# Top-k rounds over 136 candidate pairs, with key numbers found by a difference and a minimum of magnitudes

## The chip, the cores and the metric

The kernel runs on one core of one Trainium2 chip. The metric is the device time of one launch in microseconds. Engines are named as in the profile: PE is TensorE, DVE VectorE, ACT ScalarE, POOL GpSimd, SP SyncE. They run side by side, each in its own order, and meet at semaphores.

## The reference

One layer over 640 tokens of width 1024 (512 of a prompt, 128 of eight running streams) in float32. First a mixing half (a gated unit and a linear recurrence), then a retrieval half, in which each token picks experts by product keys. Of the retrieval, per head of eight:

```
v1, i1 = top_k(s1, 16)                  # s1, s2: 128 scores each
v2, i2 = top_k(s2, 16)
cand   = v1[:, None] + v2[None, :]      # 16 x 16 = 256 sums
cidx   = i1[:, None] * 128 + i2[None, :]
top_s, sel = top_k(cand, 16)
eidx   = cidx[sel];  g = softmax(top_s)
out   += sum_k g_k * gelu(u_tab[eidx_k] . x) * v_tab[eidx_k]
```

So each token has 8 x 16 = 128 expert numbers, and each number stands for a row of two tables of 16384 x 1024. Both lists v1 and v2 come sorted, largest first. A final norm follows.

## The kernel before

The tokens are five tiles of 128, worked in three "fronts": front 0 is tile 0 (the streams), front 1 tiles 1 and 2, front 2 tiles 3 and 4. Each front runs the mixing half (called I in the order), then "rounds" (II), which choose the expert numbers. Front 0 has 4 rounds, fronts 1 and 2 have 8 each, 20 in all. A round covers two heads of one tile or one head of two tiles, so always two groups ("units") of 128 tokens side by side along the free axis.

Once numbers are known, POOL gathers rows by indirect DMA into a ring of six places (line 614: a row of both tables, 8 KB per partition; line 616: a row of the first table alone, 4 KB). DVE takes dot products with the gathered rows (lines 892 and 903), ACT makes the coefficients, and the weighted sum goes to PE (line 1476) or to DVE (line 912). Tiles 1 and 2 are "dense": their second half runs over the whole second table, brought in 128 blocks of 512 KB by SP (line 568), against a coefficient matrix that is built by one-hot products (DVE lines 952 and 954, PE line 1450, multiplied at line 1461). For each half of that table 32 fills are followed by 64 blocks.

The order of all pieces is one list made by `weave` (due times written out by hand), and every engine goes through the list in that order. Each engine therefore does what is its own in a fixed sequence; a late piece holds all behind it on its engine.

A round has ten steps; step number `at` on DVE: 5 and 6 find the best sixteen of the scores for each unit (`best_keys`), 7 is `best_sums`, 8 is `next_sums`, 9 is `pick_numbers` and then `weights`. In front 0's first round the steps stand next to each other; elsewhere dot products and other pieces lie between them.

- `best_sums`: two instructions make the 256 sums of each unit (line 835). Then for each unit the eight largest (line 817), their places (820), and a copy with these taken out (823).
- `next_sums`: the next eight and their places, without line 823; the negated maximum (line 845), on which ACT's exponential and PE's score products of the next round wait; then the place is split into row and column (848, 849), and compared with 0 to 15 (851), which gives a 0/1 mask of 64 x 16 values.
- `pick_numbers`: the mask is multiplied by the key numbers (864), summed over 16 (867), and the two key numbers are put together to an expert number (870; also 875 for front 1). POOL waits for that.

`st.step` counts an instruction; `st.after` makes DVE wait until the last counted one has finished.

Of the kernel before, what the change touches and what calls it, by code (L numbers as in the profile page):

```python
# [7 lines left out]
U32 = mybir.dt.uint32  # L8
ALU = mybir.AluOpType
ACT = mybir.ActivationFunctionType  # L10
AX_X = mybir.AxisListType.X

P = 128
# [10 lines left out]
HEADS = 8  # L24
TOPK = 16
SLOTS = HEADS * TOPK
PAIRS = SLOTS // 2
RING = 6
DIAGS = 4
# [54 lines left out]
def weave():  # L84
# [8 lines left out]

    for s in range(SLOTS // 2):
        put.append((1.2 * s, ("dot", s)))
# [8 lines left out]
    b, u = 77.0, 0  # L104
    for i in range(SLOTS // 2):
        put.append((b, ("dot", SLOTS // 2 + i)))
        put.append((b + 1.11, ("mix", SLOTS // 2 + i)))
        b += 1.2
# [6 lines left out]
    put.append((b + 4.02, ("norm", 0)))  # L115
    while u < SLOTS:
        put.append((b, ("udot", u)))
# [169 lines left out]
def hybrid_layer(nc, x_all, cols, conv_state, lru_state, w_in, w_out, w_q, ws_t, w_a, w_i, keys_t, rows, experts,  # L287
                 y_all, v_rows, state_sample, state_prompt):
    with ExitStack() as ctx:
        def sb(name, shape, dt=F32):  # L290
            return ctx.enter_context(nc.sbuf_tensor(name, [P] + shape, dt))
# [29 lines left out]
        pick = sb("pick", [D])  # L321
# [13 lines left out]
        iota = sb("iota", [P])  # L335
# [14 lines left out]
        vals = sb("vals", [2, 2, TOPK])  # L350
        idx8 = sb("idx8", [2, 2, TOPK], U32)
        best = sb("best", [2, TOPK])
        sel = sb("sel", [2, TOPK], U32)
        selu = sb("selu", [2, 2, TOPK], U32)
        e12 = sb("e12", [2, 2, TOPK])
        nmax = sb("nmax", [2])
        gexp = sb("gexp", [2, TOPK])
# [8 lines left out]
        diag = sb("diag", [DIAGS, P])  # L366

        srow = pick[:, 0:2 * P].rearrange("p (e k) -> p e k", e=2)
        cand = pick[:, 0:512].rearrange("p (h k) -> p h k", h=2)
        left = pick[:, 512:1024].rearrange("p (h k) -> p h k", h=2)  # L370
        eqm = pick[:].rearrange("p (k a) -> p k a", a=TOPK)
        ws_s = pick[:, 0:GROUPS * P].rearrange("p (g n) -> p g n", g=GROUPS)

# [245 lines left out]
        def _(v):  # L619
            st = Steps(v, dve_step, dve_held)  # L620
            V = nc.vector
# [15 lines left out]
            for k in (15, 13, 11, 9, 7, 5, 3):  # L637
                v.wait_ge(dve_set, done)
                V.scalar_tensor_tensor(out=lt[:, 4], in0=lt[:, 4], scalar=1.0 / k, in1=lt[:, 3], op0=ALU.add,
                                       op1=ALU.mult).then_inc(dve_set, 1)  # L640
# [3 lines left out]
                                   op1=ALU.mult).then_inc(dve_set, 1)  # L644
# [4 lines left out]
                                   op1=ALU.add).then_inc(dve_set, 1)  # L649
# [182 lines left out]

            def best_sums():
                st.after()
                made = [st.step(V.tensor_tensor(cand[:, h].rearrange("p (a b) -> p a b", a=TOPK),
                                                vals[:, h, 0].unsqueeze(2).to_broadcast([P, TOPK, TOPK]),
                                                vals[:, h, 1].unsqueeze(1).to_broadcast([P, TOPK, TOPK]), ALU.add))
                        for h in range(2)]
                top_eight(0, [cand[:, 0], cand[:, 1]], [best[:, 0], best[:, 1]], [sel[:, 0], sel[:, 1]],
                          [left[:, 0], left[:, 1]], made)  # L840

            def next_sums(f, r):
                top_eight(1, [left[:, 0], left[:, 1]], [best[:, 0], best[:, 1]], [sel[:, 0], sel[:, 1]], None,
                          [st.last, st.last])
                guard = st.gives(V.tensor_scalar(nmax[:], best[:, :, 0], -1.0, None, ALU.mult), best_done,
                                 ROUND_BASE[f] + r + 1)
                v.wait_ge(*guard)
                st.step(V.tensor_scalar(selu[:, :, 0], sel[:], 4, None, ALU.logical_shift_right))
                st.step(V.tensor_scalar(selu[:, :, 1], sel[:], TOPK - 1, None, ALU.bitwise_and))
                st.after()  # L850
                st.step(V.tensor_tensor(eqm, selu[:].rearrange("p h e k -> p (h e k)").unsqueeze(2).to_broadcast(
                    [P, 4 * TOPK, TOPK]), iota[:, 0:TOPK].unsqueeze(1).to_broadcast([P, 4 * TOPK, TOPK]), ALU.is_equal))

            def by_unit(t, f, r):

# [3 lines left out]
                return t[:, a:a + 2, r * TOPK:(r + 1) * TOPK]  # L859

            def pick_numbers(f, r):
                eq4 = eqm.rearrange("p (q k) a -> p q k a", q=4)
                st.after()
                st.step(V.tensor_tensor(eq4, eq4, idx8[:].rearrange("p h e a -> p (h e) a").unsqueeze(2).to_broadcast(
                    [P, 4, TOPK, TOPK]), ALU.mult))
                st.after()
                st.step(V.tensor_reduce(e12[:].rearrange("p h e k -> p (h e k)"), eqm, AX_X, ALU.add))
                st.after()
                out = eid[:] if f == 1 else by_unit(idc, f, r)
                ins = V.scalar_tensor_tensor(out=out, in0=e12[:, :, 0], scalar=float(P), in1=e12[:, :, 1], op0=ALU.mult,  # L870
                                             op1=ALU.add)
                if f == 1:
                    st.step(ins)
                    st.after()
                    ins = V.tensor_scalar(by_unit(idc, f, r), eid[:], 2.0, None, ALU.mult)
                st.gives(ins, idx_ready, ROUND_BASE[f] + r + 1)
# [672 lines left out]
```

## Time and profile before

| | us |
|---|---|
| three runs, median | 1841.43 (1837.32 to 1843.55) |
| profiled execution, its time | 1844.83 |
| profiled execution, its span | 1842.6 |
| PE busy | 1470.5 (80%) |
| DVE busy | 1464.2 (79%) |
| POOL busy | 783.0 (42%) |
| ACT busy | 635.5 (34%) |
| HBM read | 671.61 MB |

Busy time is the sum of the instructions of an engine. The page has, beside it, the span cut into 40 slices of 46 us with each engine's busy share, the granted clock of PE and the DMA rate; the costliest groups of instructions; and the chain that ended last, followed back from the last instruction to what released it each time. Several engines are near four fifths busy, so the stretches have to be looked at one by one.

### The profile page before, as it was taken

To read this page: it belongs to the slowest core of one execution; us is meant where nothing else is said; L and a number is where in the kernel's file an instruction comes from. 1 tells how busy PE (TensorE), PEld (TensorE's weight loads), DVE (VectorE), ACT (ScalarE), POOL (GpSimd) and SP (SyncE) were. 2 spreads that over 40 slices of the span, in tenths; PEclk is the share of its full clock that TensorE was granted. 3 is DMA by queue.
4 is the path that set the end of the run, shared out by engine and by line. 5 is a ranking of instruction groups with operands and counts; after the bars stand their busy time and mean duration, and the time that the engine had idled before them with its cause. 6 is when DMAs were issued, how large, how long until landed. Compare 5 with 4: busy or idle time off the path is not lost.

```text
span 1842.6 us, 17478 instructions
## 1 busy us (share of the span) xinstructions
PE 1470.5 (80%) x4706; PEld 797.9 (43%) x4706; DVE 1464.2 (79%) x2979; ACT 635.5 (34%) x1935; POOL 783.0 (42%) x667
## 2 busy tenths in 40 slices
PE   6799796666666651976868999899998888999997
PEld 5485343433333210733745555333334555433332
DVE  1278788999998969769999989997667989766665
ACT  4335534222222221250037877221114667311111
POOL 2023233475776668748733334322222444422220
PEclk9899898887777785988979999999999888999999
DMA  9389999899999999999979989999998999999996
GB/s 353 144 325 409 373 353 375 317 376 381 399 379 394 365 409 371 392 344 366 406 277 331 344 313 350 418 417 417 417 417 335 362 351 370 400 417 417 417 417 250
DMA packets 146482, 675.78 MB, mean 367 GB/s; under 512 B 15216, under 2 KB 15472, under 8 KB 97232
## 3 DMA queue, kind: packets, MB, share of 16 engines
q0 software_dynamic: 92832, 538.39, 74.8%
q1 hardware_dynamic: 50496, 132.68, 18.7%
q10 hardware_dynamic: 3056, 3.61, 0.6%
q8 instruction: 37, 0.61, 0.1%
q14 instruction: 61, 0.50, 0.1%
HBM read 671.61 MB, written 3.01 MB: 366 GB/s over the span
## 4 chain that ended last, share of the span: by engine, by line
DMA 30%; PE 29%; DVE 21%; issue 10%; ACT 7%; POOL 2%; ACTq 0%; DVEq 0%; POOLq 0%; SPq 0%
DMA arena<-experts 20%; DMA ring<-experts,idc 10%; PE accY L1476 7%; PE pb L1461 7%; DVE ring L903 6%; PE pb L1281 4%; DVE ring L892 4%; PE pb L1290 2%; PE pb L1450 2%; ACT arena L1206 2%; PE pq L1407 2%; PE pb L1299 2%; DVE arena L952 2%; PE pb L1306 2%; POOL ring L616 1%
## 5 line engine op out<-in xcount | busy, mean ns | idle before, releaser
L614 POOL DMA_INDIRECT ring<-experts,idc x384 | 445.7, 1161 | 892.3 <-DVE xt L912 393.3
L1476 PE MATMUL accY<-ring,diag 128*128 128x512 f32 x792 | 458.9, 715 | 217.9 <-ACT diag L1192 217.6
L892 DVE CUSTOM_DVE_ANT_0 ring<-ring,h 128x1024 f32<-128x1024 f32 x384 | 466.6, 1222 | 194.3 <-DMA ring<-experts,idc 193.5
L1461 PE MATMUL pb<-arena 128*128 128x512 f32 x1024 | 473.0, 607 | 21.0 <-DMA arena<-experts 14.4
L616 POOL DMA_INDIRECT ring<-experts,idc x256 | 327.1, 1278 | 121.4 <-issue 76.0
L1181 ACT ACTIVATE ge<-zt 128x1 f32<-128x1 f32 x384 | 76.7, 200 | 790.9 <-DVE zt L892 789.3
L1476 PEld LDWEIGHTS accY<-ring,diag 128*128 128x128 f32 x792 | 160.3, 220 | 431.8 <-ACT diag L1192 294.5
L1461 PEld LDWEIGHTS pb<-arena 128*128 128x128 f32 x1024 | 186.3, 191 | 306.1 <-issue 196.4
L912 DVE SCALAR_TENSOR_TENSOR xt<-ring,coef,xt 128x1024 f32<-128x1024 f32 x186 | 238.4, 1282 | 6.5 <-ACT coef L1185 6.4
L1407 PE MATMUL pq<-arena 128*128 128x256 f32 (+1 forms) x768 | 153.2, 360 | 8.8 <-ACT arena L1176 4.7
L903 DVE CUSTOM_DVE_ANT_0 ring<-ring,arena 128x1024 f32<-128x1024 f32 x128 | 152.9, 1220 | 8.5 <-DMA ring<-experts,idc 7.9
L903 DVE CUSTOM_DVE_ANT_0 ring<-ring,h 128x1024 f32<-128x1024 f32 x128 | 151.5, 1221 | 8.1 <-DMA ring<-experts,idc 7.0
L1206 ACT ACTIVATE arena<-arena,qT 128x64 f32<-128x64 f32 x512 | 129.1, 334 | 80.5 <-DVE arena L954 80.5
L1450 PEld LDWEIGHTS pb<-arena 128*128 128x128 f32 x1024 | 131.6, 201 | 40.5 <-issue 31.6
L1407 PEld LDWEIGHTS pq<-arena 128*128 128x128 f32 x768 | 134.2, 204 | 34.4 <-issue 19.8
L1450 PE MATMUL pb<-arena 128*128 128x64 f32 x1024 | 128.1, 281 | 3.9 <-ACT arena L1206 3.9
L1185 ACT ACTIVATE coef<-ge,gc 128x1 f32<-128x1 f32 x384 | 113.3, 295 | 12.6
L952 DVE TENSOR_TENSOR arena<-iota,qT 128x1024 f32<-128x1024 f32 x64 | 78.1, 1221 | 14.7 <-PE pb L1450 14.7
L1192 ACT ACTIVATE diag<-ident,coef 128x128 f32<-128x128 f32 x198 | 79.6, 402 | 6.5
L1271 PE MATMUL pb<-ident,arena 128*128 128x128 f32 x100 | 18.9, 362 | 74.2 <-ACT arena L1044 53.5
L1281 PE MATMUL pb<-arena 128*128 128x256 f32 (+1 forms) x384 | 74.3, 357 | 3.3 <-ACT arena L1051 3.3
L1290 PE MATMUL pb<-arena 128*128 128x512 f32 x144 | 66.1, 616 | 6.3 <-ACT arena L1093 6.3
(174 smaller groups left out, 1123.8 us busy)
## 6 DMA issues: line engine op xcount, KB each, us to landing
arena<-experts SPq DMA_DIRECT2D x128, 512.0 KB, 15.1
arena<-w_q SPq DMA_DIRECT2D x12, 2048.0 KB, 19.5
arena<-w_in SPq DMA_DIRECT2D x11, 2048.0 KB, 20.7
ring<-experts,idc POOLq DMA_INDIRECT x640, 9.2
arena<-w_out SPq DMA_DIRECT2D x4, 2048.0 KB, 21.0
ring<-w_out SPq DMA_DIRECT2D x2, 2048.0 KB, 21.6
xt<-x_all SPq DMA_DIRECT2D x5, 512.0 KB, 13.5
y_all<-xt ACTq DMA_DIRECT2D x5, 512.0 KB, 3.5
```

The source lines that it names most:

```text
L614: nc.gpsimd.indirect_dma_start(ring[:, at // 2], None, experts, index).then_inc(gat[at], 16)
L616: nc.gpsimd.indirect_dma_start(half(g), None, halves, index).then_inc(gat[at], 16)
L892: V.tensor_tensor_reduce(out=half(g), in0=half(g), in1=h2[:], scale=1.0, scalar=0.0, op0=ALU.mult, op1=ALU.add, accum_out=zt[:, s % 8:s % ...
L903: V.tensor_tensor_reduce(out=half(g), in0=half(g), in1=h, scale=1.0, scalar=0.0, op0=ALU.mult, op1=ALU.add, accum_out=zd[:, u:u + 1]).then ...
L912: V.scalar_tensor_tensor(out=x, in0=ring[:, PLACE["whole", s][0] // 2, D:2 * D], scalar=coef[:, s % 8:s % 8 + 1], in1=x, op0=ALU.mult, op1 ...
L952: V.tensor_tensor(hot2[:, k % 2], iota[:].unsqueeze(1).to_broadcast([P, BATCH, P]), idT[:, 1, a].unsqueeze(2).to_broadcast([P, BATCH, P]), ...
L1206: ins = A.activation(hot1[:, k % 2, i], hot1[:, k % 2, i], ACT.Copy, scale=idT[:, 2, n * BATCH + i:n * BATCH + i + 1])
L1281: ins = T.matmul(pflat[:, o:o + w], wt[:, c, m * P:(m + 1) * P], hT[:, c, 0:w], start=c == 0, stop=c == DC - 1)
L1407: ins = T.matmul(pq[:, q * w:(q + 1) * w], wt[:, c, o:o + P], h2T[:, c, 0:w], start=c == 0, stop=c == DC - 1)
L1450: ins = T.matmul(pb[:, k % 4, i * BLOCKS:(i + 1) * BLOCKS], hot2[:, k % 2, i], hot1[:, k % 2, i], start=True, stop=True)
L1461: ins = T.matmul(pb[:, 2 * j + k], cm[:, i, j * P:(j + 1) * P], vring[:, n % VRING, k * 512:(k + 1) * 512], start=i == 0, stop=i == BLOCKS ...
L1476: ins = T.matmul(accY[:, j], diag[:, (n - 1) % DIAGS], ring[:, place, D + j * 512:D + (j + 1) * 512], start=first, stop=final)
```

## The change

The sums of a unit are cut from 256 to 136 columns: 16 for the largest v1 with all v2, and 8 for each of the other fifteen v1 with the first eight v2. A sum at row a and column b (from 0) can be among the sixteen largest only where (a + 1)(b + 1) is at most 16. The place in this list is split differently, and the key number is found in another way: each key number is stored with 256 times its row added (`tagged`), the wanted row times 256 is subtracted, and of the sixteen differences the one of the smallest magnitude is the key number.

```diff
+CANDS = TOPK + (TOPK - 1) * 8
+        row8 = sb("row8", [2, 2, TOPK], U32)
+        tagged = sb("tagged", [4, TOPK])
-        cand = pick[:, 0:512].rearrange("p (h k) -> p h k", h=2)
-        left = pick[:, 512:1024].rearrange("p (h k) -> p h k", h=2)
+        cand = pick[:, 0:2 * CANDS].rearrange("p (h k) -> p h k", h=2)
+        left = pick[:, 512:512 + 2 * CANDS].rearrange("p (h k) -> p h k", h=2)
 best_sums:
-                made = [st.step(V.tensor_tensor(cand[:, h].rearrange("p (a b) -> p a b", a=TOPK),
-                                                vals[:, h, 0].unsqueeze(2).to_broadcast([P, TOPK, TOPK]),
-                                                vals[:, h, 1].unsqueeze(1).to_broadcast([P, TOPK, TOPK]), ALU.add))
-                        for h in range(2)]
+                st.step(V.tensor_tensor(cand[:, :, 0:TOPK], vals[:, :, 0, 0].unsqueeze(2).to_broadcast([P, 2, TOPK]),
+                                        vals[:, :, 1], ALU.add))
+                made = st.step(V.tensor_tensor(
+                    cand[:, :, TOPK:].rearrange("p h (a b) -> p h a b", b=8),
+                    vals[:, :, 0, 1:].unsqueeze(3).to_broadcast([P, 2, TOPK - 1, 8]),
+                    vals[:, :, 1, 0:8].unsqueeze(2).to_broadcast([P, 2, TOPK - 1, 8]), ALU.add))
+                made = [made, made]
 next_sums, behind the negated maximum:
-                st.step(V.tensor_scalar(selu[:, :, 0], sel[:], 4, None, ALU.logical_shift_right))
-                st.step(V.tensor_scalar(selu[:, :, 1], sel[:], TOPK - 1, None, ALU.bitwise_and))
+                st.step(V.tensor_scalar(row8[:, :, 0], sel[:], 0xF8, 5, ALU.bitwise_and, ALU.logical_shift_left))
+                st.step(V.tensor_scalar(row8[:, :, 1], sel[:], 7, 8, ALU.bitwise_and, ALU.logical_shift_left))
+                st.step(V.scalar_tensor_tensor(out=tagged[:], in0=iota[:, 0:TOPK].unsqueeze(1).to_broadcast(
+                    [P, 4, TOPK]), scalar=256.0, in1=idx8[:].rearrange("p h e a -> p (h e) a"), op0=ALU.mult,
+                    op1=ALU.add))
                 st.after()
-                st.step(V.tensor_tensor(eqm, selu[:].rearrange("p h e k -> p (h e k)").unsqueeze(2).to_broadcast(
-                    [P, 4 * TOPK, TOPK]), iota[:, 0:TOPK].unsqueeze(1).to_broadcast([P, 4 * TOPK, TOPK]), ALU.is_equal))
+                st.step(V.tensor_scalar(selu[:, :, 0], row8[:, :, 0], 256.0, 256.0, ALU.max, ALU.subtract))
+                st.step(V.tensor_scalar(selu[:, :, 1], row8[:, :, 0], 256.0, 2048.0, ALU.is_equal, ALU.mult))
+                st.after()
+                st.step(V.tensor_tensor(selu[:, :, 1], selu[:, :, 1], row8[:, :, 1], ALU.bitwise_or))
+                st.after()
+                st.step(V.tensor_tensor(eqm.rearrange("p (q k) a -> p q k a", q=4),
+                                        tagged[:].unsqueeze(2).to_broadcast([P, 4, TOPK, TOPK]),
+                                        selu[:].rearrange("p h e k -> p (h e) k").unsqueeze(3).to_broadcast(
+                                            [P, 4, TOPK, TOPK]), ALU.subtract))
 pick_numbers:
-                eq4 = eqm.rearrange("p (q k) a -> p q k a", q=4)
                 st.after()
-                st.step(V.tensor_tensor(eq4, eq4, idx8[:].rearrange("p h e a -> p (h e) a").unsqueeze(2).to_broadcast(
-                    [P, 4, TOPK, TOPK]), ALU.mult))
-                st.after()
-                st.step(V.tensor_reduce(e12[:].rearrange("p h e k -> p (h e k)"), eqm, AX_X, ALU.add))
+                st.step(V.tensor_reduce(e12[:].rearrange("p h e k -> p (h e k)"), eqm, AX_X, ALU.min,
+                                        apply_absolute_value=True))
```

The order list, the gathers, the fills and all other pieces are the same in both kernels.

## Rows read from the trace of the kernel before

**Rows 1.** The page: busy time of the engines, DMA rate in 40 slices.

```profile
PE 1470.5 (80%) x4706; PEld 797.9 (43%) x4706; DVE 1464.2 (79%) x2979; ACT 635.5 (34%) x1935; POOL 783.0 (42%) x667
...
GB/s 353 144 325 409 373 353 375 317 376 381 399 379 394 365 409 371 392 344 366 406 277 331 344 313 350 418 417 417 417 417 335 362 351 370 400 417 417 417 417 250
```

**Rows 2.** Stretches: us, busy PE PEld DVE ACT POOL, PE clock, DMA share, GB/s.

```profile
109.00:345.00 236.00, 195.65 (x678) 117.42 (x678) 192.09 (x445) 100.91 (x256) 74.07 (x65) 0.91 0.95 372
345.00:640.00 295.00, 187.91 (x433) 92.04 (x431) 274.89 (x724) 72.47 (x205) 207.26 (x151) 0.77 0.98 377
860.00:950.00 90.00, 67.30 (x292) 56.76 (x293) 85.79 (x207) 9.42 (x17) 59.52 (x50) 0.86 1.00 389
950.00:1150.00 200.00, 180.37 (x798) 112.38 (x797) 185.83 (x428) 145.26 (x503) 77.41 (x62) 0.95 0.87 318
1150.00:1255.00 105.00, 97.20 (x227) 40.61 (x226) 102.39 (x232) 24.70 (x78) 31.13 (x28) 0.98 1.02 417
1255.00:1400.00 145.00, 140.54 (x306) 54.54 (x305) 92.97 (x115) 23.35 (x82) 37.06 (x38) 1.00 1.02 417
```

**Rows 3.** DVE groups by form: out<-in xcount, busy us, mean ns, idle before.

```profile
L912 DVE SCALAR_TENSOR_TENSOR xt<-ring,coef,xt 128x1024 f32<-128x1024 f32 x186 | 238.4, 1282 | 6.5 <-ACT coef L1185 6.4
...
L820 DVE FIND_INDEX8 sel<-best,pick 128x8 uint32<-128x256 f32 x80 | 32.5, 419 | 0.0
...
L817 DVE MAX8 best<-pick 128x8 f32<-128x256 f32 x80 | 29.9, 416 | 0.3
...
L820 DVE FIND_INDEX8 idx<-vals,psc 128x8 uint32<-128x128 f32 x80 | 22.3, 291 | 0.6 <-issue 0.6
...
L823 DVE MATCH_REPLACE8 pick<-vals,psc 128x128 f32<-128x128 f32 x80 | 21.9, 281 | 0.0
L817 DVE MAX8 vals<-pick 128x8 f32<-128x128 f32 x80 | 21.1, 290 | 0.5 <-DVE vals L817 0.5
...
L823 DVE MATCH_REPLACE8 pick<-best,pick 128x256 f32<-128x256 f32 x40 | 16.1, 409 | 0.0
L835 DVE TENSOR_TENSOR pick<-vals 128x256 f32<-128x256 f32 x40 | 15.1, 419 | 0.1
...
L849 DVE TENSOR_SCALAR selu<-sel 128x32 uint32<-128x32 uint32 x20 | 4.6, 229 | 0.0
L882 DVE TENSOR_TENSOR gc<-gexp,gsum 128x32 f32<-128x32 f32 x20 | 3.9, 193 | 0.7
```

**Rows 4.** Timeline of DVE, end of front 0's first round: start us, us.

```profile
104.40 0.18 DVE L848 TENSOR_SCALAR selu<-sel 128x32 uint32<-128x32 uint32 x1
104.49 0.17 DVE L849 TENSOR_SCALAR selu<-sel 128x32 uint32<-128x32 uint32 x1
104.70 1.23 DVE L851 TENSOR_TENSOR pick<-selu,iota 128x1024 f32<-128x1024 uint32 x1
105.96 1.22 DVE L864 TENSOR_TENSOR pick<-pick,idx 128x1024 f32<-128x1024 f32 x1
107.22 1.22 DVE L867 TENSOR_REDUCE e<-pick 128x64 f32<-128x1024 f32 x1
```

**Rows 5.** The chain that ended last, pieces from four windows: start us, us.

```profile
99.62 0.48 DVE pick L835 x2
...
104.51 2.04 PE psc L1428 x8
...
928.07 1.15 DVE pick L864
...
1108.40 0.40 DVE pick L835 x2
```

**Rows 6.** Groups of POOL.

```profile
L614 POOL DMA_INDIRECT ring<-experts,idc x384 | 445.7, 1161 | 892.3 <-DVE xt L912 393.3 <-PE accY L1476 331.1 <-DVE idc L870 92.2
```

**Rows 7.** DVE's waits from 345 to 640 us: total us, times, longest.

```profile
DVE ring L892 <- DMA ring<-experts,idc: 10.4, 8, 2.0
```

**Rows 8.** DVE's waits from 860 to 1150 us.

```profile
DVE arena L952 <- PE pb L1450: 8.3, 4, 3.1
```

## The prediction

> **What bounds the kernel now.** The page comes first [rows 1]: TensorE (PE) and VectorE (DVE) are each busy for about four fifths of the span, and DMA moves 367 GB/s on average, so no engine alone sets the time. The changed code runs on DVE only, so the question is where DVE's time is the span's time. The view of busy time by stretches answers it [rows 2]. From 1150 on, and above all from 1255 to 1400, the DMA rate stands at 417 GB/s throughout while DVE is idle a third of the time: that is the transfers' ceiling here, and nothing that DVE saves is worth anything there. From 345 to 640 DVE is busy 274.9 of 295 us and DMA moves 377 GB/s, 10% under the ceiling: both are close. From 860 to 1150 DVE is busy 271.6 of 290 us, and from 950 on DMA is far below its ceiling (318 GB/s) while PE is busy 180 of 200. From 109 to 345 DVE (81%), PE (83%) and DMA (372 GB/s) share the work.
>
> Of the 20 rounds, 4 (front 0) run from 94 to about 300, 8 (front 1) from 323 to 630, and 8 (front 2) from about 900 to 1252, the last three of these after 1150. So 17 of 20 rounds lie where DVE can matter.
>
> Third, the chain of waits. I asked for each round whether its three changed parts lie on the chain that ended last: the sums with the first eight (best_sums), the second eight with what follows (next_sums), and the picking of numbers (pick_numbers). Their marks in the chain are lines 835, 845 and 864. Line 835 is on it 11 times, from the first round to the one at 1108; line 845 10 times; line 864 8 times, the last at 928 [rows 5]. After the last of these (1108) the chain lies on transfers, PE and the dot products, and no part of a round is on it.
>
> **What a round saves.** Durations are from [rows 3, 4].
>
> Searches over 136 columns in place of 256: the same instructions exist at 128 and at 256 columns. A MAX8 takes 290 and 416 ns, so 0.98 ns a column and 0.118 us less for 120 columns; FIND_INDEX8 291 and 419 ns, 0.120 us less; MATCH_REPLACE8 281 and 409 ns, 0.120 us less. best_sums has two of each, next_sums two of the first two: 0.72 and 0.48 us. The sums themselves: two of 256 elements (0.838 us) become one of 32 (193 ns, as line 882) and one of 240 (402 ns, by 16 columns less than 256 at the same slope): 0.24 us less. So best_sums saves 0.96 us, the first half of next_sums 0.48.
>
> The multiplication by the key numbers (line 864) goes: from its start to the next instruction's 1.26 us. The comparison becomes a subtraction of the same 1024 elements with an unsigned operand, 1.22 us as line 851; the sum becomes a minimum of magnitudes of the same 1024, for which I take line 867's 1.22 us. No row shows a minimum with magnitudes or a broadcast in four dimensions of such a subtraction; line 864 did its own four-dimensional broadcast at 1.22. From below the bound is no change (three different passes over 1024 elements all take the same 1.22 us, so I exclude a gain); from above line 912, a three-operand pass over 1024 elements with a scalar read from memory, takes 1.28 us, 0.06 more a pass and 0.12 for the two. I take zero, nearest to three equal rows.
>
> What is added: before, lines 848 and 849 stood between nmax and the comparison, 0.30 us from the first start to the comparison's start (the second starts 0.09 us after the first, as nothing waits between them). After, three instructions without a wait between them (two of 32 elements, one of 64, the last costing some 226 ns between line 882's 32 and line 835's 256), a wait, two of 32, a wait, one of 32, a wait: 0.44 + 0.31 + 0.22 = 0.97 us with 0.03 us for each wait. That is 0.67 us more, all in next_sums, so next_sums as a whole gets 0.19 us longer. Bounds: 0.5 if two-step instructions overlap further, 1.2 if each takes line 849's mean of 229 ns and none overlaps. The new waits are on DVE's own instructions; what is queued behind them is DVE's next dot product or piece, and for it the price is counted already.
>
> Sum for a round: 0.96 + 0.48 - 0.67 + 1.26 = 2.03 us, and 40.6 us of DVE over 20 rounds. No transfer, PE or ACT instruction is added or taken away. ACT's exponentials hang on nmax, which comes 1.44 us earlier.
>
> **One thing that speaks against it.** Line 849 takes 0.17 us in the first round, before any gather, and 229 ns on average [rows 3, 4]: some of these short instructions are held, and GpSimd, which issues the gathers, is busy 42% of the span [rows 1]. The excess is 0.06 us each, so 40 more such instructions (four in a round where two were) cost at most 2.4 us in all; half of that, 0.06 us a round, I leave out as too small to matter. GpSimd's gather instruction has 1.16 us [rows 6]. The Trainium skill (SBUF — State Buffer, Who interferes with whom) says that such a scalar operation from SBUF to SBUF can take a port pair that GpSimd shares, and that whoever comes second waits for the whole instruction. By that rule at its worst, an estimate with half of that gather instruction as the wait: 40 x 0.42 x 0.58 = 10 us. The rows are at a quarter of it or less.
>
> **What of it is on the path.** Line 835's parts 11 x 0.96 = 10.6; line 845's 10 x 0.48 = 4.8, less 9 x 0.67 = 6.0 (after the first round's maximum PE takes the chain over at 104.51, so its tail is not on it); line 864's 8 x 1.26 = 10.1. Together 19.4 us. By stages: 2.0 in front 0's rounds, 2.0 in front 1's first (323 to 344), 9.9 between 345 and 640 (three, three and six marks), 5.5 in front 2's (five, three and one).
>
> Not all of that will be had, because what is next is near. Between 345 and 640 DVE already waits 10.4 us for gathers in line 892 alone [rows 7]; where a gain exceeds the slack of the transfers in flight, the wait for them grows instead. The transfers' own floor is 295 x (1 - 377/417) = 28 us below, so they take a share, not the whole. From 860 to 1150 DVE waits 8.3 us for PE's fills [rows 8] and PE has 20 us of idle time in the 200 from 950, over twice what four rounds save there, but in pieces. In front 0's stage PE has the chain at once after the first round. I take two thirds: 13 us. The tail from 1150 on is bytes at 417 GB/s and keeps its length, so 13 us earlier there is 13 us earlier at the end. The profiled execution has a span of 1842.6 and a time of 1844.8 us, 0.2% above the median 1841.4 of the runs; 1844.8 - 13 = 1831.8, and against the median 1828. Measurement can't tell less than about 0.3% (5.5 us) from no change.
>
> **Rivals.**
>
> *The transfers pace the middle.* DVE's waits from 345 to 640 grow by all it saves and the stretch gives nothing. For it: the page's 46 us slices reach 399 GB/s there, near the ceiling. Against: others are at 317 and 365 [rows 1], and DVE, 93% busy, is what else could hold them. What is left is 19.4 - 9.9 = 9.5, two thirds of it 6.4: 1835. The Trainium skill (DMA: Bandwidth & Descriptors, Where 436 GB/s comes from) says that HBM to SBUF traffic is held at about 358 GB/s for a core; by that the stretch would be over its limit already and this rival certain. The 417 GB/s of [rows 2] contradict that figure here.
>
> *All of DVE's time counts.* If DVE alone paces everything before 1150, its idle time being knock-on waits on itself, 17 x 2.03 = 34.5 us come off: 1807. For it: 94% busy between 860 and 1150. Against: its real waits for gathers and for PE.
>
> *Slower by TensorE's clock.* From 950 to 1150 the granted clock is 0.95 of 2.4 GHz and PE is busy 180 of 200 us; from 345 to 640, where PE mostly waits for DVE, it is 0.77. If the shifted order of DVE's pieces lets PE pause more at the start of the fills and it then runs there at 0.77, PE's work becomes 180 x 0.95/0.77 = 222 us, and the stretch takes 22 us more, against 13 saved: 1841 + 22 - 13 = 1850. It decides from a mean clock of 0.855 down (180 x 0.95/200). Against: less DVE work gives PE less to wait for.
>
> **How the numbers follow.** Forecast 1828, chance 0.60, its own range 1820 to 1835. The transfers' pace 0.22 (1835; a third of its cases within 0.3%). All of DVE's time 0.12. The slower clock 0.06. Faster by over 0.3%: 0.58 + 0.15 + 0.12 = 0.85; within: 0.09; slower: 0.06. The range for 8 of 10 leaves out most of the 34 us case and the slower one: 1813 to 1838. It holds the small costs' upper bound too (0.53 + 0.12 us more a round, some 17 x 0.65 x 2/3 = 7 us: 1835).
>
> **What would show it.** MAX8 and FIND_INDEX8 over the sums at 0.30 us; line 864's 24.4 us gone and DVE's busy time 41 us lower, near 1424; the short group 1.0 us from nmax's end to the subtraction; the minimum at 1.22 us. The middle stretch above 377 GB/s. The chain's hand-over to the transfers of the V blocks, now near 1150, some 13 us earlier and the length from there to the end the same 693 us. If that length changes by more than 3 us, or DVE's saved time turns up whole as waits for gathers, the prediction is wrong in its mechanism.

## The result and the profile after

Eight runs of the changed kernel have a median of 1827.24 us (1819.6 to 1831.73), against 1842.41 us for the kernel before on the same chip (1836.55 to 1847.77, eight runs): ratio 0.993, 95% interval 0.9907 to 0.9953, so faster, clear of noise. Measured once more (e9, six runs) it has 1826.89 us, ratio 0.9913 (0.9884 to 0.9943). The ratios here and below are those on record and not the quotients of the medians given beside them, which would be 0.9918 and 0.9917; by the first ratio the change gained 13 us, by the medians 15. The forecast was 1828 us. That figure came out right partly because errors in its terms offset each other, as the stages show.

The page after: busy time, and the rate of the transfers in 40 slices (the lines of [rows 1]).

```profile
PE 1470.6 (80%) x4706; PEld 800.0 (44%) x4706; DVE 1427.7 (78%) x3039; ACT 634.3 (35%) x1935; POOL 783.3 (43%) x667
...
GB/s 356 146 334 410 375 354 382 336 397 399 398 384 399 368 416 361 372 357 388 405 277 307 353 335 358 418 416 417 416 418 351 345 366 370 383 417 417 417 416 263
```

DVE's busy time fell by 36.5 us, PE's, ACT's and POOL's did not move. The slices of the middle stretch (the eighth to the fourteenth) rose from 317 to 399 GB/s to 336 to 399; the plateau at 417 is where it was.

Stretches after (columns as in [rows 2]):

```profile
345.00:640.00 295.00, 192.47 (x436) 95.11 (x436) 264.47 (x737) 73.90 (x210) 208.91 (x155) 0.78 0.99 389
...
950.00:1150.00 200.00, 180.87 (x796) 112.10 (x796) 180.92 (x455) 144.46 (x498) 78.12 (x66) 0.96 0.92 343
1150.00:1255.00 105.00, 102.07 (x241) 42.77 (x240) 91.67 (x213) 20.46 (x68) 30.55 (x28) 1.00 1.02 417
```

Against [rows 2] the middle stretch moves 389 GB/s in place of 377 with DVE 10 us less busy; from 1150 to 1255 the rate is the same 417 and DVE simply idles more. These windows stand at fixed times, so after the change they hold somewhat later work; cut at the same instructions (the marks below), the middle stretch goes from 376 to 386 GB/s.

DVE's groups by form after (columns as in [rows 3]):

```profile
L869 DVE TENSOR_TENSOR pick<-tagged,selu 128x1024 f32<-128x1024 f32 x20 | 24.7, 1237 | 0.7
L884 DVE TENSOR_REDUCE e<-pick 128x64 f32<-128x1024 f32 x20 | 24.2, 1212 | 0.0
...
L825 DVE FIND_INDEX8 sel<-best,pick 128x8 uint32<-128x136 f32 x80 | 22.5, 294 | 0.0
...
L822 DVE MAX8 best<-pick 128x8 f32<-128x136 f32 x80 | 20.0, 292 | 3.2
...
L828 DVE MATCH_REPLACE8 pick<-best,pick 128x136 f32<-128x136 f32 x40 | 11.1, 284 | 0.0
...
L842 DVE TENSOR_TENSOR pick<-vals 128x240 f32<-128x240 f32 x20 | 8.0, 401 | 0.0
...
L865 DVE TENSOR_SCALAR selu<-row 128x32 uint32<-128x32 uint32 x20 | 5.0, 252 | 0.0
```

And front 0's first round after, the timeline of DVE from the sums on (columns as in [rows 4]):

```profile
99.35 0.19 DVE L840 TENSOR_TENSOR pick<-vals 128x32 f32<-128x32 f32 x1
99.46 0.40 DVE L842 TENSOR_TENSOR pick<-vals 128x240 f32<-128x240 f32 x1
100.01 0.50 DVE L822 MAX8 best<-pick 128x8 f32<-128x136 f32 x2
...
102.78 0.15 DVE L853 TENSOR_SCALAR nmax<-best 128x2 f32<-128x2 f32 x1
102.96 0.18 DVE L858 TENSOR_SCALAR row<-sel 128x32 uint32<-128x32 uint32 x1
103.06 0.17 DVE L859 TENSOR_SCALAR row<-sel 128x32 uint32<-128x32 uint32 x1
103.14 0.22 DVE L860 SCALAR_TENSOR_TENSOR tagged<-iota,idx 128x64 f32<-128x64 f32 x1
103.39 0.18 DVE L864 TENSOR_SCALAR selu<-row 128x32 uint32<-128x32 uint32 x1
103.48 0.17 DVE L865 TENSOR_SCALAR selu<-row 128x32 uint32<-128x32 uint32 x1
103.69 0.19 DVE L867 TENSOR_TENSOR selu<-selu,row 128x32 uint32<-128x32 uint32 x1
103.92 1.23 DVE L869 TENSOR_TENSOR pick<-tagged,selu 128x1024 f32<-128x1024 f32 x1
105.18 1.22 DVE L884 TENSOR_REDUCE e<-pick 128x64 f32<-128x1024 f32 x1
106.43 0.19 DVE L888 SCALAR_TENSOR_TENSOR idc<-e 128x32 int32<-128x32 f32 x1
```

From the sums' first start to the start of the instruction that makes the expert numbers this is 106.43 - 99.35 = 7.08 us. Before, it was 8.85: the timeline of DVE there begins the sums at 99.62,

```profile
99.62 0.76 DVE L835 TENSOR_TENSOR pick<-vals 128x256 f32<-128x256 f32 x2
100.30 0.75 DVE L817 MAX8 best<-pick 128x8 f32<-128x256 f32 x2
```

and makes the numbers 1.25 us behind [rows 4], at 108.47. So this round saves 1.77 us, not 2.03. (It is the one round whose steps stand next to each other; 20 times 1.77 is 35.4 us, near the 36.5 us that DVE's busy time fell.) The step that was mis-sized is the sums: from the first start to the first MAX8 it was 0.68 us before and is 0.66 after. The busy time fell by 0.24 us, as forecast, but before, the first MAX8 waited only for its own unit's sums while the second unit's were being made; after, one instruction makes both units' sums and both MAX8 wait for its end.

**Where in the kernel the time came from.** The engines go through one written order, so the same instruction can be found in both timelines. Five marks on DVE, before:

```profile
343.81 0.19 DVE L870 SCALAR_TENSOR_TENSOR eid<-e 128x32 f32<-128x32 f32 x1
...
629.92 0.19 DVE L870 SCALAR_TENSOR_TENSOR eid<-e 128x32 f32<-128x32 f32 x1
...
954.52 1.22 DVE L952 TENSOR_TENSOR arena<-iota,qT 128x1024 f32<-128x1024 f32 x1
...
1139.35 1.22 DVE L952 TENSOR_TENSOR arena<-iota,qT 128x1024 f32<-128x1024 f32 x1
```

and after:

```profile
338.68 0.19 DVE L888 SCALAR_TENSOR_TENSOR eid<-e 128x32 f32<-128x32 f32 x1
...
615.60 0.19 DVE L888 SCALAR_TENSOR_TENSOR eid<-e 128x32 f32<-128x32 f32 x1
...
941.98 1.22 DVE L970 TENSOR_TENSOR arena<-iota,qT 128x1024 f32<-128x1024 f32 x1
...
1123.74 1.22 DVE L970 TENSOR_TENSOR arena<-iota,qT 128x1024 f32<-128x1024 f32 x1
```

They are the end of front 1's first and of its last round, and the first and the last one-hot product of the first half of the table. The fifth mark is the start of the last norm, 1837.5 and 1821.8. How much earlier each mark comes than before, in us, here and in the experiments (one profiled execution each):

| mark, time before | 343.8 | 629.9 | 954.5 | 1139.4 | end |
|---|---|---|---|---|---|
| changed kernel | 5.1 | 14.3 | 12.5 | 15.6 | 15.7 |
| changed kernel, again (e9) | 4.7 | 14.8 | 16.3 | 17.8 | 18.5 |
| only the minimum (e1) | 2.7 | 9.6 | 10.1 | 9.2 | 10.8 |
| only 136 columns (e2) | -0.2 | 2.1 | 3.2 | 4.8 | 3.4 |
| longer in front 1 (e3) | 2.4 | -2.9 | -3.9 | -1.8 | -2.0 |
| longer in front 2 (e4) | 5.5 | 16.2 | 18.7 | 9.5 | 13.4 |
| longer after 1150 (e5) | 3.9 | 11.7 | 11.5 | 14.2 | 19.0 |
| shorter in front 1 (e6) | 6.3 | 20.2 | 22.6 | 26.2 | 29.2 |
| shorter in front 2 (e7) | 4.2 | 14.0 | 16.3 | 25.5 | 25.2 |
| one instruction moved (e8) | 4.8 | 16.8 | 21.0 | 27.8 | 27.0 |
| 8 sums on DVE (e10) | 4.4 | 14.4 | 13.3 | 7.4 | 9.0 |
| 16 sums on DVE (e11) | 6.4 | 16.9 | 15.9 | 4.8 | 9.2 |

Six of these kernels (the changed one twice, e4, e5, e7, e10) have the same rounds up to 900 us (e7's first round of front 2, before the mark at 954, is already 2.3 us shorter). Among them the mark at 344 differs by 1.6 us, the one at 630 by 4.5, the one at 954 by 7.2: so much is chance from one execution to the next. Their means are 4.6, 14.2 and 14.8 us. All marks are taken against one execution of the kernel before, whose 1844.83 us is 2.4 above the median, so they show some 2 us too much in all. Read with that width, 4.6 us were won up to 344, 9.6 from there to 630, about nothing from 630 to 954, 2 to 3 from 954 to 1139 (3.1, 1.5 and, in e5, 2.7), and after it 0.1 and 0.7 in the two executions of the changed kernel. That last part scatters too: in e5 it is 4.8.

### The profile page after: what moved, and what is told of

Read it like the earlier page. It is cut to its first block, busy times and chain, and to the rows that moved or that the text cites. A ratio compares the mean times of both kernels' runs of the same rounds, so it can differ in the third digit from the quotient of the medians.

```text
span 1826.9 us, 17538 instructions
## 1 busy us (share of the span) xinstructions
PE 1470.6 (80%) x4706; PEld 800.0 (44%) x4706; DVE 1427.7 (78%) x3039; ACT 634.3 (35%) x1935; POOL 783.3 (43%) x667
## 4 chain that ended last, share of the span: by engine, by line
PE 32%; DMA 29%; DVE 19%; issue 10%; ACT 7%; POOL 2%; DVEq 0%; POOLq 0%; SPq 0%
DMA arena<-experts 18%; DMA ring<-experts,idc 10%; PE pb L1479 9%; PE accY L1494 8%; DVE ring L921 5%; PE pb L1299 4%; DVE ring L910 3%; PE pb L1468 2%; PE pb L1308 2%; PE pq L1425 2%; ACT arena L1224 2%; DVE arena L970 2%; PE pb L1317 2%; PE pb L1324 2%; POOL ring L621 1%
## 5 line engine op out<-in xcount | busy, mean ns | idle before, releaser
L1479 PE MATMUL pb<-arena 128*128 128x512 f32 x1024 | 473.5, 608 | 19.1 <-DMA arena<-experts 12.2
L1479 PEld LDWEIGHTS pb<-arena 128*128 128x128 f32 x1024 | 186.9, 191 | 304.1 <-issue 197.4
L921 DVE CUSTOM_DVE_ANT_0 ring<-ring,arena 128x1024 f32<-128x1024 f32 x128 | 153.4, 1220 | 11.5 <-DMA ring<-experts,idc 10.4
L921 DVE CUSTOM_DVE_ANT_0 ring<-ring,h 128x1024 f32<-128x1024 f32 x128 | 151.7, 1223 | 11.8 <-DMA ring<-experts,idc 10.9
L1468 PEld LDWEIGHTS pb<-arena 128*128 128x128 f32 x1024 | 132.6, 203 | 41.5 <-issue 31.1
L1203 ACT ACTIVATE coef<-ge,gc 128x1 f32<-128x1 f32 x384 | 113.2, 295 | 12.6
L1299 PEld LDWEIGHTS pb<-arena 128*128 128x128 f32 x384 | 66.8, 204 | 13.0 <-issue 4.4
```

The costliest lines, as they stand in the source:

```text
L921: V.tensor_tensor_reduce(out=half(g), in0=half(g), in1=h, scale=1.0, scalar=0.0, op0=ALU.mult, op1=ALU.add, accum_out=zd[:, u:u + 1]).then ...
L1299: ins = T.matmul(pflat[:, o:o + w], wt[:, c, m * P:(m + 1) * P], hT[:, c, 0:w], start=c == 0, stop=c == DC - 1)
L1468: ins = T.matmul(pb[:, k % 4, i * BLOCKS:(i + 1) * BLOCKS], hot2[:, k % 2, i], hot1[:, k % 2, i], start=True, stop=True)
L1479: ins = T.matmul(pb[:, 2 * j + k], cm[:, i, j * P:(j + 1) * P], vring[:, n % VRING, k * 512:(k + 1) * 512], start=i == 0, stop=i == BLOCKS ...
```

## The experiments

All ratios are to the kernel before on the same chip, medians with 95% intervals. "Pass" is one instruction over 1024 elements.

### e1: only the finding by a minimum

```diff
# against the changed kernel: sums and searches at 256 columns as before, and
+ st.step(V.tensor_scalar(selu[:, :, 0], sel[:], 0xF0, 4, ALU.bitwise_and, ALU.logical_shift_left))
+ st.step(V.tensor_scalar(selu[:, :, 1], sel[:], TOPK - 1, 8, ALU.bitwise_and, ALU.logical_shift_left))
- # the two row8 instructions, the two selu instructions and the bitwise_or
```

> The sums stay at 256 columns; only the finding of key numbers is changed (key numbers with 256 times their row added, one subtraction, one minimum of magnitudes). In a round one pass over 1024 elements goes (1.26 us from start to start) and the short group grows by one instruction (0.13 us): 1.13 us of VectorE a round, 22.6 in all. Theory A (a microsecond of VectorE saved before 1150 us is had at about 0.45 of what 20 rounds save, as the whole change gave 15.2 us for 20 x 1.77 = 35.4): 9.7 us faster than before. Rival B (both parts are needed before anything moves, or the searches carry it all): under 4 us. Rival C (VectorE paces all up to 1150 us): 17 rounds x 1.13 = 19 us.

1836.99 us, ratio 0.9973 (0.9943 to 1.0003): about 5 us faster, an interval that touches no change. Theory A's 9.7 us lies inside the interval and so does rival B's "under 4", so the time does not choose between them; rival C's 19 us is out. From nmax to the subtraction it has 0.61 us (0.48 before), so its saving of 1.13 us a round is as worked out. Its profiled execution was one of its faster ones (1834.01 us against the median of 1836.99), and its mark at 630 is 9.6 us earlier.

### e2: only the 136 columns

```diff
# against the changed kernel: no tagged; iota256 = 256 * (0 to 15), made once
- st.step(V.tensor_tensor(eqm..., tagged..., selu..., ALU.subtract))
+ st.step(V.tensor_tensor(eqm, selu..., iota256..., ALU.is_equal))
- st.step(V.tensor_reduce(e12..., eqm, AX_X, ALU.min, apply_absolute_value=True))
+ st.step(V.tensor_tensor(eq4, eq4, idx8..., ALU.mult))
+ st.after()
+ st.step(V.tensor_reduce(e12..., eqm, AX_X, ALU.add))
```

> The sums are cut to 136 columns; key numbers are found as before with a 0/1 mask, a multiplication and a sum (three passes over 1024 elements), but from the new places. VectorE saves 1.15 us in the searches and 0.02 in the sums and pays 0.52 for splitting the places: 0.65 us a round, 13.0 in all. Theory A: 5.6 us faster than before, and e1's and this one's gains add up to the whole change's 15. Rival B (the searches carry it): 11 us or more. Rival C (VectorE paces all up to 1150 us): 17 x 0.65 = 11 us, e1 then at 19.

1838.72 us, ratio 0.9969 (0.9949 to 0.9989): 5.7 us faster by the ratio (3.1 by the medians), as theory A had it. Its first round, from the sums to the expert numbers, takes 8.21 us against 8.85, 0.64 less. The two ratios together, 0.27% and 0.31%, make 0.58%, and the whole change has 0.7 to 0.87%; within the intervals they add up. Theory C, 19 and 11 us, is out, and so is the rival that the searches carry it all. The sizes by time are too near each other's intervals to say which part gives more. By DVE's time it is the minimum (1.13 against 0.65 us a round). The marks say the same, but e1's are those of one of its faster executions and e2's of one of its slower ones (1841.42 us).

### e3 and e6: more and less of DVE in front 1's rounds

e3 repeats the last pass twice more in each round of front 1; e6 leaves out the subtraction and the minimum there and takes the first sixteen key numbers of both lists as they stand. So e6 does not compute the layer's result: it gathers other rows of the tables, as many and as large. That their places in memory play no part is assumed.

```diff
# e3, behind the minimum:
+ for _ in range(2 if f == 1 else 0):
+     st.after()
+     st.step(V.tensor_reduce(e12..., eqm, AX_X, ALU.min, apply_absolute_value=True))
# e6:
+ if f == 1:
+     return                                     # ahead of the subtraction, which is left out
...
+ if f == 1:
+     st.step(V.tensor_copy(e12..., idx8...))    # in place of the minimum
```

> The changed kernel with front 1's eight rounds made longer: the last pass of each (the minimum over 1024 elements) is done three times, 2 x 1.25 us more a round, 20 us of VectorE between 340 and 630 us. Theory A (VectorE paces the middle stretch for about three quarters of its time, as the change gained 9.2 of 7 x 1.77 = 12.4 us there): 15 us slower than the changed kernel, so within 4 us of before. Rival T (transfers pace the middle stretch): under 4 us slower than the changed kernel. Rival C (VectorE paces it all): 20 us slower than the changed kernel, 5 slower than before.

> The changed kernel without the choice of the key numbers in front 1: the subtraction and the minimum over 1024 elements are left out, and the first sixteen key numbers of both lists are paired as they stand (so other rows of the tables are gathered, as many and as large). VectorE saves 2.3 us more a round, 18.5 in all. Theory A (the transfers' floor is near: 389 of 417 GB/s between 345 and 640 us, at most 20 us to be had): about half, 9 us faster than the changed kernel. Rival T (transfers pace it already): under 3 us. Rival C: 18 us.

e3: 1844.98 us, ratio 1.0011 (0.999 to 1.0032), so some 15 us slower than the changed kernel by the first ratio and 18 by the medians, as theory A had it; rival T's "under 4" is out. e6: 1816.92 us, ratio 0.9869 (0.9845 to 0.9893), some 10 us faster than 1827. But e5 and e8, which were measured together with e6 and do the changed kernel's work but for a late dose and a moved instruction, have 1822.43 and 1823.18 us; against them e6 is only some 6 us faster. Theory A had 9 and rival T under 3, and the time lies between. With the marks, from 344 to 630 (seven rounds):

- e3 adds 7 x 2.5 = 17.5 us of DVE to the changed kernel and the stretch gets 14.5 us longer (9.2 won becomes 5.3 lost): 0.83 a microsecond.
- the change itself took 12.4 us from the kernel before and won 9.2: 0.74.
- e6 takes another 16.1 us away and wins 4.7: 0.29.

Each of these is one execution. The six with the same rounds spread over 2.9 us in this stretch, so a slope is good to about 0.2; the fall to 0.29 is clear of that, the step between 0.83 and 0.74 is not.

The waits of DVE in that stretch, 345 to 640, for e3,

```profile
DVE ring L914 <- DMA ring<-experts,idc: 11.0, 9, 2.7
```

for the changed kernel,

```profile
DVE ring L910 <- DMA ring<-experts,idc: 19.0, 19, 2.3
```

and for e6,

```profile
DVE ring L916 <- DMA ring<-experts,idc: 30.4, 31, 2.8
```

show where time that DVE no longer needs turns up. The fixed window again holds later work in the faster kernels. Between the marks themselves DVE's waits for gathers (this line and the second dot product's, line 903 in the kernel before) are 15.8 us before, 16.0 in e3, 17.1 in the changed kernel and 28.1 in e6: 11.0 more in e6, which with the 4.7 won nearly makes up the 16.1 that it saved. The stretches themselves, e3 first, show the rate going from 374 to 400 GB/s (389 in the changed kernel):

```profile
345.00:640.00 295.00, 189.02 (x422) 94.57 (x422) 274.97 (x750) 71.15 (x200) 199.65 (x149) 0.73 0.98 374
```

```profile
345.00:640.00 295.00, 194.36 (x444) 94.17 (x444) 254.03 (x736) 75.53 (x215) 201.94 (x159) 0.80 1.01 400
```

So the price of a microsecond of DVE there is no constant. It bends where DVE starts to wait for gathers, and the change sits before the bend. The rate is then near the 417 GB/s of [rows 2]; whether that ceiling or the six places of the ring hold the gathers there, no run separates. The rival that the transfers already pace the middle is out for the change, but not for much more than it. (e3 is also a warning on DVE's busy column: at 274.97 it equals that of the kernel before.)

### e4 and e7: more and less of DVE in front 2's rounds

```diff
# e4, behind the minimum:
+ for _ in range(4 if f == 2 and 1 <= r <= 4 else 0):
+     st.after()
+     st.step(V.tensor_reduce(e12..., eqm, AX_X, ALU.min, apply_absolute_value=True))
# e7: as e6, with f == 2
```

> The changed kernel with four of front 2's rounds made longer (the second to the fifth, between 950 and 1150 us): the last pass is done five times, 4 x 1.25 us more a round, 20 us of VectorE. Theory A (PE is the limit there as often as VectorE: the change gained about 2 us of 7 there): some 10 us slower than the changed kernel, with VectorE's waits for PE's fills down from 24 us. Rival C (VectorE paces it): 20 us slower. Rival P (PE paces it alone): under 4 us slower.

> The changed kernel without the choice of the key numbers in front 2 (as e6, for the third front; five of its eight rounds before 1150 us): VectorE saves 2.3 us more a round, 11.5 before 1150. Theory A (PE limits the stretch from 950 to 1150 us): 2 to 4 us faster than the changed kernel, the rest turning into VectorE's waits for PE's fills. Rival C: 11 us faster.

e4: 1833.88 us, ratio 0.9957 (0.9938 to 0.9976); e7: 1821.53 us, ratio 0.988 (0.9852 to 0.9908). (e7, like e6, does not compute the layer's result.) Against the changed kernel's 1827 that is some 7 us slower and 6 faster; against e5 and e8, measured together with e7, it is only some 1 to 2 faster. The stretch between the marks at 954 and 1139 is the surer measure (us, one execution each):

| | length | DVE busy | DVE's waits for PE's fills |
|---|---|---|---|
| before | 184.8 | 172.2 | 8.3 |
| changed kernel | 181.8 | 164.8 | 12.9 |
| changed kernel, again (e9) | 183.4 | 164.9 | 14.2 |
| e3, e5, e6 | 182.7, 182.1, 181.2 | 165.0, 164.8, 165.4 | 11.7, 15.0, 8.4 |
| e8 | 178.0 | 164.0 | 9.3 |
| e4 | 194.0 | 184.3 | 4.3 |
| e7 | 175.7 | 156.2 | 12.7 |

e3, e5 and e6 have the changed kernel's rounds there, so five executions have the same work, 182.2 us on average. The change's own 4 x 1.77 = 7.1 us brought 2.6. As far as the one execution of the kernel before tells, most of the rest is in the last column: the wait for fills [rows 8] rose from 8.3 to 12.4 us on average. e4's 20 us more cost 11.8, 0.6 a microsecond, and the wait fell to 4.3: DVE did part of the added work in time in which it had waited. e7's 4 x 2.3 = 9.2 us less brought 6.6, 0.7 a microsecond, and the wait stayed. So the fills do take a share, as theory A had it for e4; for e7 it had 2 to 4 us and more waits, and that isn't seen. How far single executions can be off is shown by e8: with one instruction moved its stretch is 4 us shorter. The lines of the wait, 860 to 1150 us as in [rows 8], for the changed kernel,

```profile
DVE arena L970 <- PE pb L1468: 12.9, 6, 4.2
```

and for e4:

```profile
DVE arena L974 <- PE pb L1472: 6.0, 5, 1.7
```

### e5: more of DVE after 1150 us

```diff
# behind the minimum:
+ for _ in range(3 if f == 2 and r >= 5 else 0):
+     st.after()
+     st.step(V.tensor_reduce(e12..., eqm, AX_X, ALU.min, apply_absolute_value=True))
```

> The changed kernel with front 2's last three rounds made longer (after 1150 us, where the transfers run at 417 GB/s): the last pass is done four times, 3 x 1.25 us more a round, 11.2 us of VectorE. Theory A (transfers alone set the time there): no change against the changed kernel, within 2 us in the length from 1150 us to the end. Rival C (VectorE is busy 92 of 105 us there and its order holds the ring's places): up to 11 us slower.

1822.43 us, ratio 0.9891 (0.987 to 0.9911): 11.2 us more of DVE in these three rounds cost nothing. The stretch:

```profile
1150.00:1255.00 105.00, 102.52 (x245) 44.19 (x244) 103.65 (x232) 22.51 (x74) 29.54 (x28) 1.00 1.02 417
```

DVE is busy 103.65 of 105 us, more than in any other kernel here, and the rate is the same 417 GB/s. The busiest engine of a stretch isn't its limit when the transfers run at their ceiling. One part of the expectation failed: the length from the hand-over to the transfers of the second table's blocks (at 1134.22 us in the changed kernel) to the end, expected within 2 us of the changed kernel's 692.7, is 688.0. Over all kernels here it runs from 688.0 to 694.1. Nor is that tail all transfers at the ceiling: the page has slices of 335 to 370 GB/s in it before [rows 1], where the second half's fills are made, and the first to the last one-hot product of that half takes 167.6 to 174.7 us (169.0 before). e5's rounds say nothing about what DVE's time is worth there.

### e8: one instruction moved

```diff
- st.step(V.scalar_tensor_tensor(out=tagged[:], ...))        # ahead of the two selu instructions
- st.step(V.tensor_scalar(selu[:, :, 1], row8[:, :, 0], 256.0, 2048.0, ALU.is_equal, ALU.mult))
- st.after()
+ split = st.step(V.tensor_scalar(selu[:, :, 1], row8[:, :, 0], 256.0, 2048.0, ALU.is_equal, ALU.mult))
+ st.step(V.scalar_tensor_tensor(out=tagged[:], ...))
+ v.wait_ge(*split)
```

> The changed kernel with one instruction moved: the adding of 256 times the row to the key numbers goes behind the two instructions that split the places, where VectorE would wait. 0.14 us less a round from the negated maximum to the subtraction (0.96 to 0.82), 2.8 us of VectorE in all. Theory A: 1 to 2 us faster than the changed kernel, too little to tell by time, to be seen in the timeline of the first round. Rival B (the gap is not a wait but the start of the next instruction): no difference in the timeline.

1823.18 us, ratio 0.9902 (0.988 to 0.9924), not to be told from the changed kernel by time. The timeline of its first round:

```profile
101.75 0.18 DVE L858 TENSOR_SCALAR row<-sel 128x32 uint32<-128x32 uint32 x1
101.84 0.17 DVE L859 TENSOR_SCALAR row<-sel 128x32 uint32<-128x32 uint32 x1
102.05 0.18 DVE L861 TENSOR_SCALAR selu<-row 128x32 uint32<-128x32 uint32 x1
102.14 0.17 DVE L862 TENSOR_SCALAR selu<-row 128x32 uint32<-128x32 uint32 x1
102.23 0.22 DVE L863 SCALAR_TENSOR_TENSOR tagged<-iota,idx 128x64 f32<-128x64 f32 x1
102.36 0.18 DVE L867 TENSOR_TENSOR selu<-selu,row 128x32 uint32<-128x32 uint32 x1
102.58 1.22 DVE L869 TENSOR_TENSOR pick<-tagged,selu 128x1024 f32<-128x1024 f32 x1
```

From the first splitting to the subtraction it is 0.83 us, against 0.96 in the changed kernel: the gap was a wait, and an independent instruction fits into it.

### e9, e10, e11: is PE the limit between 954 and 1139?

e9 is the changed kernel again, as the neighbour of the other two. They move weighted sums of tile 3 from PE to DVE.

```diff
 def by_vector(s):
-    return k >= SLOTS // 2 or (t == 2 and k % 5 in (1, 3))
+    return k >= SLOTS // 2 or (t == 2 and k % 5 in (1, 3)) or (t == 1 and k % 8 == 3)   # e10
+    return k >= SLOTS // 2 or (t == 2 and k % 5 in (1, 3)) or (t == 1 and k % 4 == 3)   # e11, on e8
```

> The changed kernel as it is, once more, so that the next kernels have it beside them on the same chip. From its first measurement: 0.993 of before, about 13 us; from the three kernels that differ least from it (a late dose, a moved instruction) 0.989 to 0.990. I expect 0.990 to 0.993.

> The changed kernel with 8 of the first 64 weighted sums of tile 3 (between 950 and 1150 us, every eighth) moved from PE to VectorE: PE gives up 8 x 1.73 = 13.8 us there, VectorE takes on 8 x 1.28 = 10.2 us. Theory P (PE's matmuls limit that stretch; e4 put 20 us more on VectorE there for some 5 to 7 us): 4 to 10 us faster than the changed kernel. Rival V (VectorE limits it as much): no change or up to 10 us slower. Rival L (the chain of one-hot, scaling and fill limits it, not the sums): no change.

> As e10 with 16 sums moved (every fourth), and the adding of the row moved behind the splitting as in e8: PE gives up 27.7 us between 950 and 1150, VectorE takes on 20.5. Theory P: VectorE is now the limit; about as e10 or a few us worse, 0 to 8 us faster than the changed kernel. Rival V: 10 to 20 us slower.

e9: 1826.89 us, 0.9913 (0.9884 to 0.9943), as expected. e10: 1833.14 us, 0.9951 (0.9933 to 0.997). e11: 1834.42 us, 0.9946 (0.9921 to 0.9971). Theory P, which was mine, falls: neither got faster. Rival L's "no change" isn't seen either. Rival V fits e10, 6 us slower than e9; for e11 it had 10 to 20, and by time e11 is 7.5 slower, though its stretch is 13 to 14 longer. The stretch between the two marks, for the changed kernel, e10 and e11:

```profile
942.00:1123.80 181.80, 167.56 (x745) 105.00 (x746) 164.86 (x399) 136.67 (x478) 68.82 (x58) 0.96 0.88 324
```

```profile
941.20:1131.90 190.70, 163.68 (x719) 103.74 (x720) 174.11 (x406) 134.89 (x473) 73.59 (x58) 0.91 0.83 310
```

```profile
938.60:1134.60 196.00, 161.32 (x689) 104.62 (x690) 182.34 (x414) 132.40 (x466) 69.35 (x58) 0.87 0.83 307
```

10.2 us more on DVE made it 8.9 us longer (7.3 against e9). In e11, of whose 16 sums 15 lie between the marks, 19.2 us made it 14.2 longer (12.6 against e9, but 17.9 against e8, whose order of instructions it has). PE gave up 13.8 and 27.7 us of matmuls by the price of one at full clock, but its busy time fell by 3.9 and 6.2 us only: its mean clock, the last number but two of a line, went from 0.96 to 0.91 and 0.87. So PE at 92% busy was not the limit by its matmuls: taking some away and putting less on DVE made the stretch longer, by about what e4's dose on DVE alone would (0.6 a microsecond there, 0.7 to 0.9 here). DVE is the limit for most of its time. No run takes work from PE alone, and whether the lower clock, by slower fills, has a part in the longer stretch is not separated.

## Why the prediction was right, and where its terms were not

- **The limit by stretches: shown.** Added time on DVE counts for most of itself from 344 to 630 (e3), for 0.6 and more between 954 and 1139 (e4, e10), and for nothing in the three rounds after 1150 (e5).
- **Searches, 0.120 us an instruction: shown**, a little more (292, 294, 284 ns against 416, 419, 409 in [rows 3]).
- **The sums, 0.24 us: mis-sized.** 0.02 by starts. The overlap of two independent instructions with the first search was lost, and the forecast had subtracted busy times.
- **The two remaining passes at 1.22 us: shown** (1.237 and 1.212). The multiplication's 1.26 is gone.
- **The short group, 0.67 us more: shown** in the first round, 0.96 against 0.30. Over all rounds line 865 means 252 ns and line 864 207, against 0.17 and 0.18 in the first round. That is at most 0.08 us on an instruction (the other short ones are within 0.02), so the rule of the Trainium skill (SBUF — State Buffer, Who interferes with whom), which I had put at up to 10 us, is not seen at that size; with 20 x (0.08 + 0.03) = 2.2 us the rows stay at about a fifth of it. No run here takes the gathers away to show whose hold it is.
- **DVE's sum, 40.6 us: 35.4** by starts (20 x 1.77), 36.5 by busy time.
- **Two thirds of 19.4 us, 13: mis-sized, by luck in the right direction.** 13 us came by the ratio and 15 by the medians, but with other parts. With the sums at 0.02 the parts on the chain are not 19.4 but 17.0 us (11 x 0.22 less), and two thirds of that would be 11. Up to 344 4.6 us came where two thirds of 4.0 was meant, and from 344 to 630 9.6 where 6.6 was: no less than the chain's parts, which with the smaller sums are 3.3 and 9.2. In front 2's stretch 2 to 3 came in place of 3.7, somewhat over half of its 4.4. (The marks count some 2 us too much in all, as said there.) So one share for all stages was the mistake. The larger yield made good the smaller saving of a round. Why so much came early is not shown; that DVE's parts off the chain help too, since what is queued behind them starts earlier, is a guess.
- **The tail keeps its length: shown for the changed kernel; its reason only in part.** The chain's hand-over to the blocks' transfers moved from 1149.65 to 1134.22 us, 15.4 us, and from it to the end of the span there are 692.9 and 692.7 us. "Bytes at 417 GB/s" holds for much of it, not for the second half's fills (see e5), and over all kernels the length scatters by 6 us.
- **PE as what is next after 950: half right.** DVE's wait for PE's fills did grow, by some 4 us (the table at e4), and that is most of what the change saved there and did not win. But PE's idle time, read in the prediction as the slack, does not tell it: e10 and e11 take matmuls from PE, its clock falls, and nothing is won.
- **The rivals.** The transfers pace the middle: out for the change, which won 9.6 us there; they come into play soon behind it (e6). All of DVE's time counts: out, by the changed kernel's 15 us of 30 (17 x 1.77) and by e6's bend. The clock rival: not seen, the changed kernel has 0.96 there, and no loss; e11 shows that 0.87 can come from taking work off PE.

The hand-over to the blocks' transfers in the chain of waits, before and after:

```profile
1149.65 8.37 DMA arena<-experts
```

```profile
1134.22 8.23 DMA arena<-experts
```

Of the versions that do all the work none is clearly faster than the changed kernel; e8 is at least as fast, its first round is 0.13 us shorter, and it is the one to keep.

## What to carry to other kernels

Price an edit by starts, not by busy times: where two instructions ran one behind the other without a wait, merging them can cost the overlap that they had with their users. Then ask in each stretch what a microsecond of the engine is worth, and measure it from both sides, by repeating a pass and by leaving one out: it was 0.83, 0.74 and 0.29 in one stretch as the waits for gathers grew, and 0 in another at 99% busy. That a second engine looks 90% busy does not make it the limit: take work from it and look.

## What the runs showed that was not expected

PE's busy time hardly follows its work when DVE paces it: 28 us of matmuls less left its busy time 6 us lower, at a mean clock of 0.87 in place of 0.96. And the scatter of single executions is built up stage by stage: with the same instructions up to 900 us, the mark at 344 spreads over 1.6 us, at 630 over 4.5, at 954 over 7.2. A stage's own length, between two marks, scatters less (2.9 us from 344 to 630, 2.2 from 954 to 1139 over the five with the same rounds), but it takes several executions to trust a difference of a few us: e8's second of these stretches is 4 us off the others.
